# Two heads of a pair side by side in the attention products, and the third layer's log-forget products behind them

## The reference, cut to what matters

```python
# sliding window (layers 1 and 4)
scores = jnp.einsum('bnqkgd,bnskd->bnkgqs', qb, kk).astype(jnp.float32) * (hd ** -0.5)
...
out = jnp.einsum('bnkgqs,bnskd->bnqkgd', probs.astype(vv.dtype), vv)
# forgetting attention (layer 3), query block i of 128, keys up to its end
s = jnp.einsum('bhqd,bhkd->bhqk', q[:, :, t0:t1], k[:, :, :t1]).astype(jnp.float32) * (hd ** -0.5)
s = s + lc[:, :, t0:t1, None] - lc[:, :, None, :t1]
mask = jnp.arange(t1)[None, :] <= (t0 + jnp.arange(blk))[:, None]
p = jax.nn.softmax(jnp.where(mask[None, None], s, -jnp.inf), axis=-1)
outs.append(jnp.einsum('bhqk,bhkd->bhqd', p.astype(v.dtype), v[:, :, :t1]))
```

## Time and profile before

| what | value |
|---|---|
| median of 3 runs | 1644.21 us (1643.32 to 1651.99) |
| span of the profiled execution | 1646.8 us |
| mean granted PE clock | 0.987 of full speed |
| PE busy | 1584.8 us, 96% |
| PEld busy | 1499.3 us, 91% |
| DVE busy | 1196.7 us, 73% |
| ACT busy | 792.2 us, 48% |
| POOL busy | 95.2 us, 6% |
| transfers | 383.76 MB, mean 233 GB/s |

### The profile page before, as it was taken

One profiled execution on the slowest core, in us unless ns is written; L12 is line 12 of the kernel. 1 busy time (PEld: TensorE's weight loads), 2 busy tenths in 40 slices (PEclk: granted clock), 3 DMA queues, 4 the chain that ended last, 5 costly groups with the idle time before them and its releaser, 6 DMA issues.

```text
span 1646.8 us, 30909 instructions
## 1 busy us (share of the span) xinstructions
PE 1584.8 (96%) x12544; PEld 1499.3 (91%) x12553; DVE 1196.7 (73%) x1723; ACT 792.2 (48%) x1042; POOL 95.2 (6%) x105
## 2 busy tenths in 40 slices
PE   2989999999999999999999999999999999999998
PEld 1868999999989999988899999889999899889998
DVE  6898877778468777854587777868777687676665
ACT  2555333366364343544454335565333467654543
POOL 0150000001000000011000000120000012200000
PEclk9989999999999999999999999999999999999999
DMA  9855978755257878562458876445888645345550
GB/s 391 333 205 201 372 292 311 280 207 183 71 205 315 314 292 326 222 215 103 156 226 337 318 305 240 141 165 228 334 320 307 228 157 176 119 145 197 178 178 26
DMA packets 54220, 383.76 MB, mean 233 GB/s; under 512 B 6256, under 2 KB 6512, under 8 KB 8448
## 3 DMA queue, kind: packets, MB, share of 16 engines
q1 hardware_dynamic: 50400, 363.75, 58.5%
q0 software_dynamic: 3744, 18.94, 3.3%
HBM read 378.47 MB, written 4.19 MB: 232 GB/s over the span
## 4 chain that ended last, share of the span: by engine, by line
PE 85%; DVE 9%; DMA 3%; ACT 2%; issue 1%; POOL 1%; SPq 0%; DVEq 0%; ACTq 0%
PE PS L1905 69%; PE PS L1926 4%; DVE wlo L1354 3%; PE PS L2047 2%; DMA CST<-cst_in 1%; PE PS L1972 1%; DVE adar L1372 1%; DMA adar<-ada 1%; PE PS L1936 1%; ACT whi L944 1%; DVE SCR L1526 1%; PE PS L2073 1%; PE PS L2094 1%; DMA raw<-ada 1%; PE PS L1946 1%
## 5 line engine op out<-in xcount | busy, mean ns | idle before, releaser
L1905 PE MATMUL PS<-hhi,whi 128*128 128x256 f32 x2496 | 717.1, 287 | 4.9 <-DVE hlo L564 2.4
L1354 DVE TENSOR_TENSOR wlo<-raw,whi 128x2048 fp32r<-128x2048 f32 x234 | 537.1, 2296 | 251.0 <-ACT whi L944 250.6
L1905 PE MATMUL PS<-hlo,whi 128*128 128x256 f32 x2496 | 710.3, 285 | 0.0
L1905 PE MATMUL PS<-hhi,wlo 128*128 128x256 f32 x2496 | 710.0, 284 | 0.0
L944 ACT ACTIVATE whi<-raw 128x2048 fp32r<-128x2048 f32 x234 | 447.3, 1912 | 493.0 <-PE PS L1905 481.1
L1905 PEld LDWEIGHTS PS<-hhi,whi 128*128 128x128 f32 x2496 | 483.0, 194 | 13.8 <-issue 10.5
L1905 PEld LDWEIGHTS PS<-hlo,whi 128*128 128x128 f32 x2496 | 483.3, 194 | 1.3 <-issue 1.2
L1905 PEld LDWEIGHTS PS<-hhi,wlo 128*128 128x128 f32 x2496 | 483.2, 194 | 0.0
L1372 DVE CUSTOM_DVE_ANT_0 adar<-adar,CB 128x1024 f32<-128x1024 f32 x232 | 276.9, 1233 | 7.4 <-DMA adar<-ada 7.4
L1905 PE MATMUL PS<-ahi,whi 128*128 128x256 f32 x968 | 274.5, 284 | 1.1 <-DVE alo L1855 1.1
L1905 PE MATMUL PS<-alo,whi 128*128 128x256 f32 x968 | 273.9, 283 | 0.0
(11 more groups left out here) (235 smaller groups left out, 1386.5 us busy)
## 6 DMA issues: line engine op xcount, KB each, us to landing
raw<-weights SPq DMA_DIRECT2D x234, 1024.0 KB, 6.3
adar<-ada SPq DMA_DIRECT2D x104, 1024.0 KB, 5.6
adar<-ada POOLq DMA_DIRECT2D x12, 1024.0 KB, 5.4
raw<-ada SPq DMA_DIRECT2D x4, 1024.0 KB, 15.2
bias_rows<-acc POOLq DMA_DIRECT2D x12, 256.0 KB, 3.6
adar<-bias_rows POOLq DMA_DIRECT2D x8, 256.0 KB, 3.1
CST<-cst_in SPq DMA_DIRECT2D x1, 1128.0 KB, 22.7
CB<-c_in SPq DMA_DIRECT2D x2, 512.0 KB, 3.9
```

The lines of the kernel that those rows point to most:

```text
L1354: v.tensor_tensor(wlo[:, u % CV, :], raw[:, u % RAW, :], whi[:, u % CV, :].bitcast(F32), ALU.subtract).then_inc(lo_done, 1)
L1905: m = pe.matmul(o, w(a), h(b), start=first and k_ == 0, stop=last and k_ == 2, skip_group_check=True)
```

## The change

In `scores` the loop over the query tiles is now outside and the loop over the two heads inside, so that head 0 and head 1 follow each other for each tile. The log-forget products of the third layer are taken out of that loop and stand behind all four score products of the pair, in the order of before (head, then tile, `LCQ` then `LCK`). In `values` the loop over the key tiles is now outside and the loop over the heads inside. The products themselves, their operands, the waits ahead of them and the signals behind the last of them are the same.

```diff
-                    for h in range(2):
-                        r = slice(64 * h, 64 * h + 64)
-                        o = bank[4 + h]
-                        kt = p // 4 + 2 * ((p // 2 + h) % 2) if kind == "swa" else p
-                        for q in range(2):
-                            if kind == "b2":
-                                n, part = S, o[:, S * q:S * q + S]
-                            else:
-                                n = P * (q + 1)
-                                part = o[:, P * q:P * q + n]
-                            m = pe.matmul(part, QT[r, p, P * q:P * q + P], KT[r, kt, 0:n], start=q == 0, stop=kind != "fox", skip_group_check=True)
-                            if kind == "fox":
-                                sel = SEL[:, 2 * p + h:2 * p + h + 1]
-                                pe.matmul(part, LCQ[:, P * q:P * q + P], sel.to_broadcast([P, n]), start=False, stop=False, skip_group_check=True)
-                                m = pe.matmul(part, sel.to_broadcast([P, P]), LCK[:, 0:n], start=False, stop=True, skip_group_check=True)
+                    def part(h, q):
+
+                        return bank[4 + h][:, S * q:S * q + S] if kind == "b2" else bank[4 + h][:, P * q:P * q + P * (q + 1)]
+
+                    for q in range(2):
+                        n = S if kind == "b2" else P * (q + 1)
+                        for h in range(2):
+                            r = slice(64 * h, 64 * h + 64)
+                            kt = p // 4 + 2 * ((p // 2 + h) % 2) if kind == "swa" else p
+                            m = pe.matmul(part(h, q), QT[r, p, P * q:P * q + P], KT[r, kt, 0:n], start=q == 0, stop=kind != "fox", skip_group_check=True)
+                    if kind == "fox":
+                        for h in range(2):
+                            sel = SEL[:, 2 * p + h:2 * p + h + 1]
+                            for q in range(2):
+                                pe.matmul(part(h, q), LCQ[:, P * q:P * q + P], sel.to_broadcast([P, P * (q + 1)]), start=False, stop=False, skip_group_check=True)
+                                m = pe.matmul(part(h, q), sel.to_broadcast([P, P]), LCK[:, 0:P * (q + 1)], start=False, stop=True, skip_group_check=True)
                     m.then_inc(s_ready, 1)
...
                     o, pt = value_bank(p), probs_t(kind)
-                    for h in range(1 if is_diff(kind, p) else 2):
...
-                        pe.matmul(o[r, :], V[:, 0, col:col + w], pt[:, h, 0:S], start=True, stop=False, skip_group_check=True)
-                        if kind == "b2":
-                            m = pe.matmul(o[r, :], V[:, 1, col:col + w], pt[:, h, S:2 * S], start=False, stop=True, skip_group_check=True)
-                        else:
-                            m = pe.matmul(o[r, P:S], V[:, 1, col:col + w], pt[:, h, S:S + P], start=False, stop=True, skip_group_check=True)
+                    for t in range(2):
+                        for h in range(1 if is_diff(kind, p) else 2):
...
+                            q0 = 0 if t == 0 or kind == "b2" else P
+                            m = pe.matmul(o[r, q0:S], V[:, t, col:col + w], pt[:, h, S * t:S * t + S - q0], start=t == 0, stop=t == 1, skip_group_check=True)
                     m.then_inc(pv_done, 1)
```

More of the change, by code:

```diff
@@ L2087, in values @@
                     o, pt = value_bank(p), probs_t(kind)
-                    for h in range(1 if is_diff(kind, p) else 2):
-                        if is_diff(kind, p):
-                            r, w, col = slice(0, P), P, P * p
-                        else:
-                            r, w = slice(64 * h, 64 * h + 64), HD
-                            col = HD * (p // 2 if kind == "swa" else 2 * p + h)
-                        pe.matmul(o[r, :], V[:, 0, col:col + w], pt[:, h, 0:S], start=True, stop=False, skip_group_check=True)
-                        if kind == "b2":
-                            m = pe.matmul(o[r, :], V[:, 1, col:col + w], pt[:, h, S:2 * S], start=False, stop=True, skip_group_check=True)
-                        else:
-                            m = pe.matmul(o[r, P:S], V[:, 1, col:col + w], pt[:, h, S:S + P], start=False, stop=True, skip_group_check=True)
+                    for t in range(2):
+                        for h in range(1 if is_diff(kind, p) else 2):
+                            if is_diff(kind, p):
+                                r, w, col = slice(0, P), P, P * p
+                            else:
+                                r, w = slice(64 * h, 64 * h + 64), HD
+                                col = HD * (p // 2 if kind == "swa" else 2 * p + h)
+                            q0 = 0 if t == 0 or kind == "b2" else P
+                            m = pe.matmul(o[r, q0:S], V[:, t, col:col + w], pt[:, h, S * t:S * t + S - q0], start=t == 0, stop=t == 1, skip_group_check=True)
                     m.then_inc(pv_done, 1)
```

## The result

The changed kernel takes 1632.32 us as the median of 4 runs (1629.92 to 1634.37), against 1646.22 us of 4 runs of the kernel before (1643.32 to 1651.99). The ratio is 0.9909 with a 95% interval of 0.9887 to 0.9931, so the change makes the kernel faster by about 0.9%. The forecast was 1630.0 within 1626 to 1637, and 14.2 us less than before; the two medians lie 13.9 us apart, and the ratio makes it 15.0. The interval of the ratio reaches from 11.4 to 18.6 us, so that the medians come within 0.3 us of the forecast is luck; the trace has to tell what the change gave.

The account below looks back on a forecast made before the run. PE, busy 96% of the span, was taken to bound the kernel. Savings of 13.5 us in the third layer's score blocks and 0.7 us from PE's clock take the median from 1644.2 to 1630.0 us, range 1626 to 1637.

Parts of the forecast that it names:

- the sign of it: Span from the first third-layer score to the start of the feed-forward net was to be 13 to 15 us shorter.
- The third layer's block: Each of eight third-layer score blocks was to take 1.77 us instead of 3.46, saving 13.5 us in all.
- the lower bound: Third layer's run of eight log-forget products at 0.108 us each, 0.86 us; the forecast took 0.91.
- The borrowed price: Third layer's four score products priced at 0.86 us, from the same shapes in the first layer, instead of 2.07.
- Other blocks: Scores in the first, fourth and fifth layers (24 blocks) and all values (32 blocks) were to gain 0.
- The waits: Third layer: PE's only wait for another engine, 1.0 us before values(5), was to stay, with no new ones.
- The margin of pair 0: Third layer: pair 0's probabilities leave POOL 9.8 us before their transposes; one shorter block was to take 1.69 of it.
- The clock: PE's clock fall in the third layer cost 1.4 us; the forecast took half, 0.7 us, as saved.
- Rival 1: Third layer: heads overlap less than borrowed, or log-forget products keep their old price; 1640 or 1636 us, chance 0.07.
- Rival 2: Third layer: another engine takes up the gain, a shorter block becoming a wait; 1641 to 1644 us, chance 0.05.
- Rival 3: Other layers' scores and values: heads do not overlap yet, so they gain 20.7 us; 1609 in all, chance 0.04.
- Rival 4: 24 score blocks that overlap now: alternating halves makes each product wait for the one before; 1671 us, chance 0.04.

Follow-up runs that it names:

- e1: Kernel before the change with the new order in the third layer's scores alone: 1631.61 us, 0.9917 of before.
- e3: Changed kernel with scores and values back to head after head, third layer's log-forget products still behind all four score products: 1634.28 us, 0.9928 of before.
- e4: Changed kernel with the third layer's four log-forget products of each query tile right behind that tile's two score products: 1636.68 us, 0.9931 of before.
- e5: Changed kernel with each head's third-layer log-forget products on the same 64 rows as its scores, sums and selector held twice: 1627.86 us, 0.9887 of before.
- e6: Changed kernel with first- and fourth-layer scores head after head and a 16-row product of zeros between the heads: 1646.35 us, 1.0 of before.
- e8: Data of e5, but everything head after head, each score product followed by its two log-forget products: 1633.62 us, one run.
- e2: Changed kernel with the third layer's scores put back as before the change, new order everywhere else: 1647.09 us, 0.9992 of before.

## Why the prediction was right

**The bound.** That time taken out of PE's work in the third layer would come out of the total held: all that follows the layer starts earlier by what the blocks and the clock gave, and e1, with the third layer's edit alone, has the ratio of the whole change. The 15.2 us that came out of the layer lie just above the 13 to 15 that were to be the sign of it, mostly by the half of the clock's fall that the forecast left out.

**The third layer's block.** Forecast 1.77 us, of which 0.86 for the scores and 0.91 for the log-forget products; measured 1.75, 0.86 and 0.89. The loads of the run are 0.11 us apart throughout, nearer to the lower bound than I took. The saving is 1.71 a block and 13.7 in all, against 13.5. The borrowed price, of the same four products in the first layer, was the right row.

**Other blocks.** Forecast 0; measured 0.006 us less in each, 0.3 us in all, far below what can be told.

**The waits.** Forecast none new, and the 1.0 us before values(5) to stay; both held (1.1). The margin of pair 0 shrank by 3.2 us and not by 1.7, since I had counted one shorter block, but not that the probabilities would gain next to nothing from the other, because DVE was still busy when the scores came. It cost nothing here; with a margin of 3 us it would have.

**The clock.** I took half of 1.4 us. The third layer has no fall in the profile of the changed kernel, nor in those of e1, e3, e4, e5, e6 and e8, whose blocks take 1.3 to 2.1 us; both profiles with blocks of 3.46 us, of the kernel before and of e2, have one, in different blocks. So the whole 1.4 was probably the better value. One profile of each kernel does not settle it. The reason that the forecast gave for the fall, short pieces with waits between them, does not stand in the rows: PE waited for no other engine there, and PEld stood idle for 0.17 us ahead of the scores. What made the clock fall is not shown.

**The rivals.** Rival 1 (less overlap): the block itself speaks against it. Rival 2 (another engine takes up the gain): no new wait. Rival 3 (the heads elsewhere do not overlap yet): e2 gains nothing, and e6 shows what those layers would have cost if it were so. The sentence of the Trainium skill (TensorE: Matmul & The Clock Gate, section Part 3: Packing small matmuls) on strict order of matmuls, on which that rival stands, is not what these runs show: in e3 (84.57, ahead of 85.05) and in e8 (712.88, ahead of 712.90 and 712.92) head 1's matmuls start ahead of matmuls of head 0 that precede them in the program. Rival 4 (alternation ends the overlap): the blocks of the other layers kept their time.

What the forecast had not said: in the third layer too the side-by-side order is worth nothing that can be measured; with the log-forget products moved, head after head does as well (e3, 1.76 us a block against 1.75).

## What to carry to other kernels

Look for a product with another number of rows between products that use different halves of the array: here most of its price was not its own time but the overlap that it ended and the changes of rows on both sides (1.71 of 2.60 us a block, the rest being 0.89 for the run of eight). Sort such a block by the rows that its products use, or better give the odd products the same halves as their neighbours. Before you reorder for overlap, compare the order of lines in the trace with the order in the program: PE may overlap already, in these runs with up to three matmuls of the other half still to start.

## What the runs showed of the hardware that I had not expected

- PE starts matmuls out of the order of the program where they use another half of the array (of its rows in the scores, of its columns in the values), and in these runs so far ahead that three matmuls of the first half are still to start: with four matmuls a head the second head starts at once (0.86 us, e3), with eight it starts 0.50 us late, at the fifth (1.80 instead of 1.31 us, e8 and e5).
- One head alone in a block of four score matmuls takes as long as two, 0.85 us (e6): a product of 64 rows leaves the other half of the array free for the other head.
- Products that stand in the trace as one matmul each overlap in the two halves like the 32-bit ones, which stand as two (e5): eight log-forget products add 1.31 - 0.86 = 0.45 us to the block, against 0.89 in a run with all rows.
